# Where updates and publishings of x stand in the memory key and value projection of a two-stack transformer kernel

## What is computed

```
def memory_cross_attention(h, m, w_q, w_kv, w_o):
    q = (h @ w_q).reshape(bsz, seq, MEM_HEADS, MEM_HEAD_DIM)
    k, v = jnp.split(m @ w_kv, 2, axis=-1)
    ...
    s = jnp.einsum("bqhd,bkhd->bhqk", q, k) * (MEM_HEAD_DIM ** -0.5)
    o = jnp.einsum("bhqk,bkhd->bqhd", softmax(s), v).reshape(bsz, seq, D_MODEL)
    return o @ w_o

for layer in range(2):
    h = rmsnorm(x, g_mix_pre[layer])
    y = fox_shortconv_mixer(h, ...) if layer == 0 else rglru_mixer(h, ...)
    x = x + rmsnorm(y, g_mix_post[layer])
    h = rmsnorm(x, g_cross_pre[layer])
    m = rmsnorm(mem, g_mem[layer])
    y = memory_cross_attention(h, m, w_xq[layer], w_xkv[layer], w_xo[layer])
    ...
```

## Time and profile before

| | |
|---|---|
| median of three runs | 2903.58 us (2890.7 to 2905.81) |
| span of the profiled execution | 2899.1 us (its own time beside the span is not given) |
| mean granted TensorE clock | 0.972 |
| PE, PEld busy | 2756.2 us (95%), 2249.2 us (78%) |
| DVE, ACT, POOL busy | 1071.8 us (37%), 1094.1 us (38%), 1348.0 us (46%) |
| weight loads | 462 of 512 KB |

### The profile page before, as it was taken

The page is one execution under the profiler, slowest core; times in us unless marked ns, Lnnn a source line. Parts: engine busy times, 40 slices in busy tenths (PEclk is TensorE's granted clock), DMA queues, the critical chain, the costliest instruction groups (busy, mean ns, idle before and its releaser), DMA issues.

```text
span 2899.1 us, 37907 instructions
## 1 busy us (share of the span) xinstructions
PE 2756.2 (95%) x13516; PEld 2249.2 (78%) x13516; DVE 1071.8 (37%) x1941; ACT 1094.1 (38%) x1777; POOL 1348.0 (46%) x715
## 2 busy tenths in 40 slices
PE   7999999999989999999988999999988889999998
PEld 5756888888857888878757887888876788788886
DVE  5674322112663222124445334221055673332212
ACT  5665333223664323232253334322236443333221
POOL 4545444444475444444354544444443364454442
PEclk9999999999999999999989999999999999999999
DMA  4300323333302332332202312333322231232331
GB/s 157 124 2 30 102 94 95 102 107 100 94 9 69 94 101 92 104 102 85 90 22 94 126 51 73 101 96 99 108 81 66 95 127 55 66 102 94 101 102 65
DMA packets 69090, 251.79 MB, mean 87 GB/s; under 512 B 7672, under 2 KB 7928, under 8 KB 68736
## 3 DMA queue, kind: packets, MB, share of 16 engines
q1 hardware_dynamic: 67104, 244.35, 26.4%
q10 hardware_dynamic: 1888, 6.14, 0.6%
HBM read 248.36 MB, written 2.10 MB: 86 GB/s over the span
## 4 chain that ended last, share of the span: by engine, by line
PE 87%; DVE 8%; issue 2%; ACT 2%; POOL 1%; DMA 0%; DVEq 0%; POOLq 0%; ACTq 0%
PE ps L565 26%; PE ps L566 26%; PE ps L567 26%; PE ps L703 4%; PE ps L728 2%; PE ps L714 2%; DVE xl L1438 1%; DVE acc L1431 1%; POOL pr L531 1%; DVE y_mid L1741 0%; DVE pr L1531 0%; PE ps L673 0%; DVE ps L1762 0%; DVE r_l L1923 0%; DVE tmpb L1920 0%
## 5 line engine op out<-in xcount | busy, mean ns | idle before, releaser
L484 POOL TENSOR_TENSOR w_lo<-w_raw,w_hi 128x1024 fp32r<-128x1024 f32 x462 | 1118.0, 2424 | 1352.3 <-ACT w_hi L1014 1352.0
L565 PE MATMUL ps<-xh,w_hi 128*128 128x512 f32 x2384 | 940.4, 394 | 42.7 <-DVE xl L1438 21.0
L566 PE MATMUL ps<-xl,w_hi 128*128 128x512 f32 x2384 | 933.7, 392 | 0.0
L567 PE MATMUL ps<-xh,w_lo 128*128 128x512 f32 x2384 | 933.3, 391 | 0.0
L1014 ACT ACTIVATE w_hi<-w_raw 128x1024 fp32r<-128x1024 f32 x462 | 484.4, 1053 | 547.0 <-PE ps L567 538.9
L565 PEld LDWEIGHTS ps<-xh,w_hi 128*128 128x128 f32 x2384 | 451.8, 190 | 141.7 <-issue 42.6
L566 PEld LDWEIGHTS ps<-xl,w_hi 128*128 128x128 f32 x2384 | 452.1, 190 | 95.0 <-issue 1.7
L567 PEld LDWEIGHTS ps<-xh,w_lo 128*128 128x128 f32 x2384 | 451.3, 189 | 94.5
L565 PE MATMUL ps<-hh,w_hi 128*128 128x512 f32 x704 | 273.9, 389 | 0.0
L566 PE MATMUL ps<-hl,w_hi 128*128 128x512 f32 x704 | 273.9, 389 | 0.0
L567 PE MATMUL ps<-hh,w_lo 128*128 128x512 f32 x704 | 273.9, 389 | 0.0
(11 more groups left out here) (259 smaller groups left out, 2901.7 us busy)
## 6 DMA issues: line engine op xcount, KB each, us to landing
w_raw<-weights_in SPq DMA_DIRECT2D x462, 512.0 KB, 3.5
x<-x_in ACTq DMA_DIRECT2D x4, 512.0 KB, 10.1
mem<-mem_in ACTq DMA_DIRECT2D x2, 1024.0 KB, 4.9
x_out<-x SPq DMA_DIRECT2D x4, 512.0 KB, 2.6
rope<-rope_in ACTq DMA_DIRECT2D x1, 512.0 KB, 12.0
tab<-tables_in ACTq DMA_DIRECT2D x2, 256.0 KB, 2.9
tab<-tables_in ACTq DMA_DIRECT2D x1, 384.0 KB, 12.4
small<-small_in ACTq DMA_DIRECT2D x1, 326.5 KB, 4.9
```

The costliest lines, as they stand in the source:

```text
L484: nc.gpsimd.tensor_tensor(w_lo[:, slot], w_raw[:, slot], w_hi.bitcast(f32)[:, slot], ALU.subtract).then_inc(lo_ready, 1)
L565: nc.tensor.matmul(dst, w_hi[:, slot, w], hi, start=first, stop=False)
L566: nc.tensor.matmul(dst, w_hi[:, slot, w], lo, start=False, stop=False)
L567: return nc.tensor.matmul(dst, w_lo[:, slot, w], hi, start=False, stop=last)
```

## The change

On VectorE `add_normed` of feature tile m // 2 now stands behind each even tile m of `xkv` and `publish` of m // 2 behind each odd one, in both layers; the nop stands directly behind the evacuation. On ScalarE `renormed(m // 2)` stands behind the rounding of each odd tile.

```
@@ ScalarE
                 for m, g in steps(f"xkv{e}"):
                     if m == 0:
                         root()
-                    if m < KT:
-                        renormed(m, f"cross_pre{e}")
+                    if m % 2:
+                        renormed(m // 2, f"cross_pre{e}")
@@ VectorE
                     scaled(k_x[:, m] if m < 8 else z_vx[:, m - 8], bank, MEM, rstd_m).then_inc(evac_done, 1)
-                    if m < KT:
-                        add_normed(y_mid, f"mix_post{e}", m)
                     dve.wait_ge(evac_done, BANK0[f"xkv{e}"] + m + 1)
                     V.engine_nop().then_inc(proj_ready, 1)
-                    if 1 <= m <= KT:
-                        publish(m - 1, f"cross_pre{e}")
+                    if m % 2 == 0:
+                        add_normed(y_mid, f"mix_post{e}", m // 2)
+                    else:
+                        publish(m // 2, f"cross_pre{e}")
```

## The result

| | before | changed |
|---|---|---|
| median (five runs each, side by side) | 2902.45 us (2890.7 to 2905.81) | 2911.64 us (2909.24 to 2917.72) |
| span of the profiled execution | 2899.1 us | 2914.6 us |
| mean granted TensorE clock | 0.972 | 0.969 |
| evacuations of `xkv0`, start of the first to start of the last | 1566.63 to 1620.67: 54.04 us | 1568.26 to 1627.60: 59.34 us |
| the same of `xkv1` | 2328.01 to 2382.77: 54.76 us | 2337.44 to 2396.77: 59.33 us |

The ratio is 1.0045, 95% interval 1.0033 to 1.0056. It compares the means of the five runs (2900.2 and 2913.2 us), which lie 13 us apart; the medians in the table lie 9.2 apart. So the change is slower by 9 to 13 us, clear of zero and just inside the half per cent that the prediction called "no change that can be told". The forecast of 2918 was 6 us above the measured median; the range held.

A forecast was written before the change was run, and what follows sets the result against it. VectorE, taking turns with GpSimd, was held to bound tiles 0 to 8, then TensorE. Per stage 5.0 us later evacuations plus 2.3 us of clock, twice, +14.6 on the median 2903.58: 2918 us, range 2901 to 2926.

The forecast's parts named there:

- step 1: On VectorE, ahead of `acc` and `xl`: a new wait for ScalarE's `xh`, 0.9 us per pair of tiles.
- The sum: Whole kernel: 5.0 us of later evacuations and 2.3 us of slow clock, in two stages, +14.6 us.
- the ring: From one `xh` over `w_hi`, two `w_lo` holding `y_mid` and `x`, to the next `xh`: 8.2 us per pair.
- step 2: On VectorE: GpSimd's `w_lo` holds `y_mid` and `x`, two blocked instructions in 5.53 us, 8.2 us per pair.
- step 3: First tiles of a stage: `y_mid` and `x` slip 0.11 us; six periods on, the last evacuation starts 5.0 us later.
- the race: Second `y_mid` against `w_lo` at the stage's start: `w_lo` comes first by 0.04 us and holds `y_mid`.
- the other outcome: Rival: the second `y_mid` starts ahead of `w_lo`, last evacuation 3.8 us late, +12.2 us, 2915.8; chance 0.15.
- step 4: Stage end: the last `acc` and `xl`, 1.3 us, fall behind tile 15 under TensorE's transposes and cost nothing.
- step 5: TensorE behind tile 15: idle 6 to 9 us, then restarts at half clock and loses 2.3 us per stage.
- no change: Rival: about every third `w_lo` holds nothing, a pair takes 7.35 us, time 2899 to 2908 us; chance 0.13.
- Faster: Rival: weights run ahead, a pair stays below 7.35 us, time 2872 or 2888 us; chance 0.10.
- More late behind it: Rival: slow clock stretches the transposes too and pairs need 8.6 us, +20 us, 2924; chance 0.15.

The follow-up runs named there:

- pub_next: The changed kernel with `acc` and `xl` of each feature tile one evacuation later; 2910.38 us, ratio 1.004.
- psum_after: The changed kernel with `rstd` and the product `y_mid` writes held in PSUM in both memory projections; 2882.59 us, ratio 0.9938.
- nop_back: The changed kernel with the nop back behind `add_normed`, as before the change; 2908.19 us, ratio 1.0028.
- pe_busy10: The changed kernel with ten extra matmuls per stage, result unused, between tile 15 and the transposes; 2909.16 us, ratio 1.0025.
- sq_after: psum_after with the squares of feature tiles 1 to 6 in PSUM too; 2868.79 us, ratio 0.9895.
- sq_before: The kernel before the change, with the same PSUM edit as sq_after; 2879.54 us, ratio 0.9934.

## Why the prediction came out as it did

*The wait that appears* (step 1) was put at 0.9 us per pair and is 0.97 or 0.98. It is there eight times per stage, the last time where it costs nothing. pub_next adds what the step did not say: this wait is a remainder and not a cost of its own. The sum was right all the same, since it was made round the ring and not by adding up waits. The chunk loads, put at nothing, cost nothing: from 1568 to 1628 us ScalarE's roundings in the changed kernel never wait for a load.

*Where `w_lo` falls* (step 2) was right as to instruction: `y_mid` and `x` are held, `acc` and `xl` free, pair 8.2 us and measured 8.22. Two sizes shift against each other. The first `w_lo` starts 1.1 behind the end of `xh`, with `y_mid` 0.66 behind its start, so `y_mid` is held to 2.37 and not to the 2.77 that was carried over; the nop's 0.12 and the changes of turn take that back. psum_after shows the cause. Outside VectorE's two-port modes, the Trainium skill (SBUF — State Buffer, "SBUF: two separate sides") restricts the block to VectorE instructions with two SBUF inputs against a GpSimd instruction that reads SBUF. `rstd`'s reciprocal, with one, ran its usual 3.35 us beside a `w_lo` that took 2.40 at 1565.95, and with one operand in PSUM `y_mid` and `x` go free, so the traces agree.

*The start* (step 3) had the race at 0.04 us for `w_lo`, and it was won by 0.05. The last evacuation was to slip by 5.0 us and slipped by 5.30 and 4.57 against each stage's own start. nop_back settles that the race was a real fork: 0.12 us the other way are worth 1.5 us per stage, not 1.2. That the forecast had the winner right was luck as much as working, since 0.04 us is less than the rows it was added up from can carry (the neighbours' overlap is 0.07); it had given the other outcome a chance of its own.

*The end* (step 4) was right: the last `acc` starts at 1628.98 and the last `xl` is over at 1630.34, under transposes that last until 1631.80.

*TensorE's clock* (step 5) was right in the place, in the 6 to 9 us of idleness (8.77) and in the size (2.3 and 1.76 for 2.3 forecast). It was made up differently: the step let ten matmuls of `xq0` run slow, but the transposes take most of it, 1.7 us, and three matmuls the rest. pe_busy10 ties it to the idleness. The Trainium skill (TensorE: Matmul & The Clock Gate, "Terms") describes the throttle as a share of pulses withheld; with half of them withheld over the 4.96 us from 1628.12 to 1633.08 the loss would by that estimate be 2.5, near the 2.3 by rows.

*The sum* was +14.6 and the rows of the two stages give 13.9; the means of the runs are 13.0 apart, their medians 9.2. The forecast of 2918 lies some 6 us above the median, and most of that is not the mechanism. About 1 us is the base, since five runs put the kernel before at 2902.45 and not at 2903.58. The other 5 us are the distance between 14.6 and the 9.2 of the medians, and the spread of five runs (2890.7 to 2905.81 and 2909.24 to 2917.72) is too wide to say which of 9.2 and 13.0 is nearer. The prediction also took the 4.5 us between span and median for a constant. In the changed kernel a run and its span lie 1.8 apart (2916.4 and 2914.6); by that the profiled execution before took an estimated 2900.9, and 14.6 more is 2915.5, against 2916.4 for the profiled execution of the changed kernel.

That the last evacuations of `xkv1` slipped by 4.57 and not 5.30 comes from the kernel before, whose second stage was 54.76 and not 54.04 us; the step took the same cost for both. VectorE is no slower there: its run of `z_vx` starts 44.54 us behind the first evacuation, in the first stage 44.57. TensorE is, in a window of the second stage before the change:

```profile
2366.00:2368.00 2.00, 2.00 (x11) 2.00 (x11) 1.89 (x3) 0.00 (x0) 2.00 (x2) 0.50 0.50 150
```

The granted clock is 0.50, where it is 1.00 at the same place of the first stage (1604 to 1608), and TensorE comes to its last tiles late. So the lower clock already cost the kernel before 0.7 us here, which the sum did not have.

Of the rivals, *no change* put too much on `w_lo` falling into VectorE's wait: none does, since GpSimd ran dry at 1577.80 (1572.59 + 5.21), ahead of that wait, and the next `w_hi` stands behind the very `xh` that VectorE waits for. *Faster* named the right price (weights beside an engine that is free of two-operand work) and was right that a pair below 7.35 us decides. psum_after, with two pairs in 12.5 us, is faster indeed, but needed an edit that the change did not bring. *More late behind it* had one thing right, the slow transposes, and its pair of 8.6 us wrong.

In a sentence: the change turns 20.6 us per stage in which VectorE is held into 26.4, in a ring that also contains ScalarE, and so bounds sixteen tiles where eight had been bound.

## What to carry to other kernels

Before work is spread over more steps, ask what it collides with there: here spreading helped once little was left to collide (sq_after against sq_before), and hurt while every pair of steps also held two whole-instruction turns of another engine. Remove the collision first (one operand in PSUM), then spread; in that sequence the placement that cost 0.45% here is part of a gain of 1.05%. And when a wait sits inside a ring, shortening it moves the idleness and not the end: measure the period, not the wait.

## What was not expected of the hardware

- A matmul of two float32 operands that were not rounded first, 512 columns, stands in the trace as two entries of 0.43 us (20 issued, 40 in 17.17 us; 10 issued, 20 in 8.75). The rounded ones of `xq` come 0.23 us apart at the same clock.
- A gap shorter than the 4.17 us of the earlier trace rows was followed by slow transposes too: in psum_after TensorE stood 3.61 us and they took 3.58; in sq_after it stood 0.6 us and they took 1.97. A longer gap was not followed by slower ones: nop_back's first had 7.29 us and 3.34. Timeline of TensorE in psum_after:

```profile
1609.06 3.58 PE L894 MATMUL ps<-ident,z_vx 128*128 128x128 f32 x16 [3.61 <-DVEq L1805]
```

- A held instruction lasts for the rest of the other's turn and then its own work: 1.41, 1.51, 2.01, 2.37 and 2.90 us have been seen for work of 0.69 or 0.75, by how late in a `w_lo` it started. GpSimd on its part took 2.40 us alone and 2.6 to 2.8 per `w_lo` when the two alternate.
